# Block 2 of a two-block fp32 network: value tiles taken in pairs, and two transpositions side by side

## What is computed

```python
for i in range(DEPTH_2):
    kind, j = i % N_MIXERS, i // N_MIXERS
    h = rms_norm(x, norm_g[i]) * (1.0 + sc[:, None]) + sh[:, None]
    hc = rms_norm(xc, norm_g[i]) * (1.0 + scc) + shc
    u, z = jnp.split(h @ w_in, [n_mix_cols], axis=-1)   # u holds q, k and v
    ...
    logits = jnp.einsum("bqhgd,bkhd->bhgqk", qb, k).astype(jnp.float32) * scale
    p = jax.nn.softmax(logits, axis=-1).astype(v.dtype)
    return jnp.einsum("bhgqk,bkhd->bqhgd", p, v)
    ...
    x = x + gt[:, None] * ((o * jax.nn.silu(z)) @ w_out)
```

## Time and profile before

| | us |
|---|---|
| median of 3 runs | 2225.64 (2219.51 to 2228.34) |
| the profiled execution | 2225.83 |
| its span in the profile | 2223.7 |
| TensorE busy | 2028.1 |
| VectorE, ScalarE, GpSimd busy | 1194.2, 1089.7, 924.8 |
| block 2 within the span | from about 936 on |

### The profile page before, as it was taken

The page is one execution under the profiler, slowest core; times in us unless marked ns, Lnnn a source line. Parts: engine busy times, 40 slices in busy tenths (PEclk is TensorE's granted clock), DMA queues, the critical chain, the costliest instruction groups (busy, mean ns, idle before and its releaser), DMA issues.

```text
span 2223.7 us, 39126 instructions
## 1 busy us (share of the span) xinstructions
PE 2028.1 (91%) x14528; PEld 1707.4 (77%) x14528; DVE 1194.2 (54%) x2582; ACT 1089.7 (49%) x2089; POOL 924.8 (42%) x582
## 2 busy tenths in 40 slices
PE   6899899988998999888999999888899989979897
PEld 5798799988988899775666797566679766657776
DVE  6854556648645566346774205666430676633563
ACT  5353466453534665454554426444441656544553
POOL 1574378104744682033443123333311545532563
PEclk9899999998999999999999999999999999989998
DMA  7343556653435666542113332321232221123221
GB/s 263 106 151 105 190 171 193 188 189 115 151 109 171 186 191 191 169 143 76 48 39 105 123 97 66 107 65 48 86 114 95 76 76 48 48 93 108 88 82 57
DMA packets 72990, 262.89 MB, mean 118 GB/s; under 512 B 8048, under 2 KB 10224, under 8 KB 72560
## 3 DMA queue, kind: packets, MB, share of 16 engines
q1 hardware_dynamic: 71536, 256.31, 36.5%
q0 software_dynamic: 1280, 4.20, 0.6%
HBM read 259.43 MB, written 1.05 MB: 117 GB/s over the span
## 4 chain that ended last, share of the span: by engine, by line
PE 65%; DVE 12%; ACT 9%; issue 8%; POOL 5%; DMA 1%; DVEq 0%; ACTq 0%; SPq 0%; POOLq 0%
PE gemm L458 15%; PE gemm L459 14%; PE gemm L460 14%; PE gemm L740 7%; PE score L781 2%; PE tbank L696 2%; PE obank L839 2%; DVE small L1771 2%; POOL w_lo L298 1%; PE stat L703 1%; POOL rot L1976 1%; ACT pr L1347 1%; ACT w_hi L1020 1%; PE score L786 1%; PE gemm L666 1%
## 5 line engine op out<-in xcount | busy, mean ns | idle before, releaser
L298 POOL TENSOR_TENSOR w_lo<-ring,w_hi 128x1024 fp32r<-128x1024 f32 x262 | 628.9, 2403 | 655.9 <-ACT w_hi L1020 654.5
L458 PE MATMUL gemm<-g_hi,w_hi 128*128 128x256 f32 x1344 | 393.3, 293 | 29.0 <-DVE w_lo L298 10.5
L1020 ACT ACTIVATE w_hi<-ring 128x1024 fp32r<-128x1024 f32 x344 | 361.2, 1053 | 81.4 <-PE gemm L460 38.0
L458 PE MATMUL gemm<-h_hi,w_hi 128*128 128x512 f32 (+1 forms) x928 | 385.3, 415 | 4.7 <-POOL w_lo L298 4.7
L459 PE MATMUL gemm<-g_lo,w_hi 128*128 128x256 f32 x1344 | 382.6, 285 | 0.0
L460 PE MATMUL gemm<-g_hi,w_lo 128*128 128x256 f32 x1344 | 382.4, 284 | 0.0
L459 PE MATMUL gemm<-h_lo,w_hi 128*128 128x512 f32 (+1 forms) x928 | 348.4, 375 | 0.0
L460 PE MATMUL gemm<-h_hi,w_lo 128*128 128x512 f32 (+1 forms) x928 | 348.0, 375 | 0.0
L458 PEld LDWEIGHTS gemm<-g_hi,w_hi 128*128 128x128 f32 x1344 | 263.2, 196 | 48.1 <-issue 23.4
L459 PEld LDWEIGHTS gemm<-g_lo,w_hi 128*128 128x128 f32 x1344 | 263.3, 196 | 0.1
L460 PEld LDWEIGHTS gemm<-g_hi,w_lo 128*128 128x128 f32 x1344 | 263.0, 196 | 0.0
(11 more groups left out here) (306 smaller groups left out, 3543.7 us busy)
## 6 DMA issues: line engine op xcount, KB each, us to landing
ring<-wall SPq DMA_DIRECT2D x478, 512.0 KB, 3.7
r<-nbias POOLq DMA_DIRECT2D x16, 256.0 KB, 2.9
cst<-consts SPq DMA_DIRECT2D x1, 2037.0 KB, 13.2
r<-x_t SPq DMA_DIRECT2D x1, 1024.0 KB, 5.8
x<-ctx_t SPq DMA_DIRECT2D x1, 1024.0 KB, 15.7
y_t<-x SPq DMA_DIRECT2D x4, 256.0 KB, 2.4
cst<-consts SPq DMA_DIRECT2D x1, 303.5 KB, 3.5
x<-pos SPq DMA_DIRECT2D x1, 128.0 KB, 2.1
```

The costliest lines, as they stand in the source:

```text
L298: eng.tensor_tensor(w_lo[:, q % SPLITS, :, :], ring[:, t % RING, :, :], w_hi[:, q % SPLITS, :, :].bitcast(F), ALU.subtract)\
L458: pe.matmul(out, w[0][:, k, :], x[0], start=start, stop=False)
L1020: act.activation(w_hi[:, q % SPLITS, :, :], ring[:, t % RING, :, :], ACT.Copy).then_inc(S["hi_ready"], 1)
```

## The change

Value tiles are split like the others and taken two at a time (`value_pair`): the token block of h is the stationary operand, both tiles together are the 256 moving columns, and each product is three fp32r passes, 96 for a pair in place of 64 plain matmuls. The first pair runs with the eight feature chunks outermost and the four token blocks in two gemm and two score banks; later pairs use two gemm banks or the banks `t2` and `tb` by turns. `SPLITS` is 4, and `split_slots` puts the tiles of a pair side by side; the fourth buffer is the old `scratch`. `t2` is the third gemm bank, so from block 2 on two banks take turns. The first two value tiles come before the adaLN rows in the plan, and in layers of kind A the second row comes after the pair. High and low parts of h are made column by column as soon as a column is scaled; GpSimd scales all eight context columns, not four.

In attention of kinds A and B, `pair_to_keys` turns both units of the previous pair right behind the scores of this one, into `tb` and `t2`, then four `gemm_part`s run in one piece, then `values_both`. VectorE and ScalarE follow in that order. Kind C keeps its order, with two gemm banks.

The diff, cut to its core:

```diff
     put("ln", 2 * DEPTH, "RRRR" * FILL[2 * DEPTH])
     for L, kind in enumerate(KINDS):
         nk = n_kv_chunks(kind)
-        put("rms", L, "RRRR" * FILL_RMS[L])
-        put("v", L, "R" * nk)
+        put("v", L, "PP" + "RRRR" * FILL_RMS[L] + "PD" * (nk > 2) + "P" * (nk - 4))
         put("q0", L, "P")
         put("k", L, "P" * nk)
...
+def v_tile(L, j):
+
+    return AT["v", L] + j + (4 * FILL_RMS[L] if j >= 2 else 0)
...
+def split_slots():
+
+    fixed = {}
+    for L, kind in enumerate(KINDS):
+        nk = n_kv_chunks(kind)
+        for j in range(nk):
+            fixed[v_tile(L, j)] = (2 + j) % SPLITS
+        fixed[AT["q0", L]] = 2 if nk > 2 else 0
+    slots, last, held = [], 0, {}
+    for t, k in enumerate(PLAN):
+        if k != "R":
+            at = fixed.get(t, (last + 1) % (SPLITS - 1))
+            slots.append((at, held.get(at, -1)))
+            held[at] = len(slots) - 1
+            last = at
+    return slots
+
...
+        G2 = 2 * FILL[0] + DEPTH * (17 + NG + 2 * KC + KC + 2 * FILL[1] + 2 * FC + KC + 2 * FILL[2])
+        t2 = gb[2]
+
+        def gemm_bank(g):
+
+            return gb[g % 3 if g < G2 else g % 2]
...
-                    pe.wait_ge(S["bank_read"], g - 2)
+                    pe.wait_ge(S["bank_read"], g - 2 if g < G2 else max(g - 1, G2))
                 n["g"] += 1
-                return gb[g % 3]
+                return gemm_bank(g)
...
-                for _ in range(FILL_RMS[L]):
-                    run(ada_row())
+                n["tile"] += 2
+                run(ada_row())
...
-                for j in range(nk):
-                    w, out = tile(), bank()
-                    for t in range(4):
-                        if j == 0 and t == 2:
-                            pe.wait_ge(S["h_ctx"], (1 + L) * KC)
+                def value_pair(j):
+
+                    t = v_tile(L, j)
+                    split_tile(t), split_tile(t + 1)
+                    a, _ = SPLIT_SLOT[int(SPLIT_NO[t])]
+                    hi, lo = w_hi[:, a:a + 2, :, :], w_lo[:, a:a + 2, :, :]
+                    if j % 4 == 0:
+                        out = [bank(), bank()]
+                    else:
+                        pe.wait_ge(S["t_read"], n["t"])
+                        if j > 2:
+                            pe.wait_ge(S["v_ready"], vbase(L) + j - 2)
+                        out = [t2, tb]
+                    if j == 0:
+                        pe.wait_ge(S["ada_evac"], n["ada"])
+                        places = [(b, 0) for b in out + sbk]
+                    else:
+                        places = [(out[i // 2], i % 2 * 2 * P) for i in range(4)]
+
+                    def part(i, k, start):
+
+                        x, (b, o) = slice(i * P, (i + 1) * P), places[i]
+                        to = b[:, o:o + 2 * P].rearrange("p (a n) -> p a n", a=2)
+                        pe.matmul(to, h_hi[:, k, x], hi[:, :, k, :], start=start, stop=False)
+                        pe.matmul(to, h_hi[:, k, x], lo[:, :, k, :], start=False, stop=False)
+                        return pe.matmul(to, h_lo[:, k, x], hi[:, :, k, :], start=False, stop=(k == KC - 1))
+
+                    if j == 0:
                         for k in range(KC):
-                            if j == 0 and t == 0:
-                                pe.wait_ge(S["h_full"], (5 + L) * KC + k + 1)
-                            ins = pe.matmul(out[:, t * P:(t + 1) * P], h2[:, k, t * P:(t + 1) * P], w[:, k, :],
-                                            start=(k == 0), stop=(k == KC - 1))
-                    tile_done(ins)
+                            h_wait(k)
+                            for i in range(4):
+                                ins = part(i, k, k == 0)
+                    else:
+                        for i in range(4):
+                            for k in range(KC):
+                                ins = part(i, k, k == 0)
+                        n["tile"] += 2
+                    ins.then_inc(S["split_done"], 2)
+
+                for j in range(0, nk, 2):
+                    value_pair(j)
...
+                    pe.wait_ge(S["p_normed"], pbase(L) + U + 2)
+                    if c == 0 and u == 0:
+                        pe.wait_ge(S["ss_used"], kbase(L) + nk - 1)
+                    pe.wait_ge(S["t_read"], n["t"])
+                    for hh in range(2):
+                        for j in range(4):
+                            ins = pe.transpose((tb, t2)[hh][:, j * P:(j + 1) * P], pr[:, (U + hh) % 3, j * P:(j + 1) * P], ident)
+                        ins.then_inc(S["t_ready"], 1)
+                    n["t"] += 2
+                    turned_at[c, u + 1] = n["t"]
...
+                    for u in range(0, NU, 2) if kind != "C" else ():
+                        last = (c, u - 2) if u else (c - 1, NU - 2)
+                        scores(c, u)
+                        if last[0] >= 0:
+                            pair_to_keys(*last)
+                        for i in range(4):
+                            if i == (2 if NU == 4 else 0) and u == NU - 2 and c + 1 < KC:
+                                q_sums(c + 1)
+                            gemm_part()
+                        if last[0] >= 0:
+                            values_both(last[0], last[1] // 2)
...
+                n["tile"] += 2
+                ada_row_out(0)
+
+                def high(m):
+
+                    act.wait_ge(S["h_full"], (5 + L) * KC + m + 1)
+                    act.wait_ge(S["h_ctx"], L * KC + m + 1)
+                    act.activation(h_hi[:, m, :], h2[:, m, :], ACT.Copy).then_inc(S["h_hi_ready"], 1)
+
                 for m in range(KC):
                     act.wait_ge(S["normed"], (5 + L) * KC + m + 1)
                     act.activation(h2[:, m, 0:T], h2[:, m, 0:T], ACT.Identity, bias=ada[:, L, m, 0:1], scale=mod[:, m, 0:1])\
                         .then_inc(S["h_full"], 1)
...
+                for j in range(0, nk, 2):
+                    if j:
+                        n["tile"] += 2
+                    hi_parts(n["tile"] - 1 + AHEAD)
+                    act.wait_ge(S["split_done"], int(SPLIT_NO[v_tile(L, j + 1)]) + 1)
+                    for i in range(2):
+                        if j % 4 == 0:
+                            n["g"] += 1
+                            b = gemm_bank(n["g"] - 1)
+                        else:
+                            b = (t2, tb)[i]
+                        if j:
+                            seq(act.activation(vv[:, 2 * i:2 * i + 2, j * P:(j + 2) * P], b[:, :].rearrange("p (t n) -> p t n", t=2), ACT.Copy))
+                        else:
+                            act.activation(vv[:, i, 0:2 * P], b[:, 0:2 * P], ACT.Copy)
+                            seq(act.activation(vv[:, 2 + i, 0:2 * P], sbk[i][:, 0:2 * P], ACT.Copy))
+                        if j % 4 == 0:
+                            act.sem_inc(S["bank_read"], 1)
...
-                        act.wait_ge(S["t_ready"], tbase(L) + c * NU + u - 2)
+                        act.wait_ge(S["t_ready"], tbase(L) + (c * NU + u - 3) // 2 * 2 + 2)
...
+                    for u in range(0, NU, 2) if kind != "C" else ():
+                        last = (c, u - 1) if u else (c - 1, NU - 1)
+                        if NU == 4 and u == 2 and c + 1 < KC:
+                            query()
+                        if last[0] >= 0:
+                            second_keys(*last)
+                        exponential(c, u)
+                        exponential(c, u + 1)
+                        if NU == 6 and u == 2:
+                            if c + 1 < KC:
+                                query()
+                            elif slot:
...
+                for m in range(KC + 3):
+                    if m < KC:
+                        dve.tensor_tensor(h2[:, m, :], x2[:, m, :], st[:, :], ALU.mult).then_inc(S["normed"], 1)
+                    if m >= 3:
+                        dve.wait_ge(S["h_hi_ready"], n["h"] * KC + m - 2)
+                        dve.tensor_tensor(h_lo[:, m - 3, :], h2[:, m - 3, :], h_hi[:, m - 3, :].bitcast(F), ALU.subtract).then_inc(S["h_ready"], 1)
                 n["h"] += 1
+                split_to(AT["q0", L] - 1)
...
+                    for u in range(0, NU, 2) if kind != "C" else ():
+                        last = (c, u - 2) if u else (c - 1, NU - 2)
+                        biggest(c, u)
+                        biggest(c, u + 1)
+                        if last[0] >= 0:
+                            first_keys(*last)
+                        if u == OT and c:
+                            gate_out(c - 1)
+                        if NU == 6 and u == 4 and c + 1 < KC:
+                            q_end(c + 1)
+                        normalise(c, u)
+                        normalise(c, u + 1)
+                        if u == 2 and c + 1 < KC:
+                            q_start(c + 1)
+                            if NU == 4:
+                                q_end(c + 1)
```

(20 more changed lines are left out.)

141 lines of the change are left out of this document (64 added, 77 removed).

## The result

The changed kernel takes 2196.78 us (median of 4 runs, 2196.49 to 2203.45) against 2224.11 before (4 runs). The ratio is 0.9858, 95% interval 0.983 to 0.9886: faster by 1.4%, 32 us, and clear of noise. (The two medians alone are 27 us apart; the interval stands for 25 to 38 us.) The forecast was 81 us, and 2196.8 lies above the end of its range, 2186. The direction was right, the size wrong by more than half.

What follows compares the result with a forecast made beforehand. TensorE, busy 91% of the span, was taken to bound the kernel. Value projection -33, attention -59 and added waits +11 sum to -81: from 2225.83 us to 2144.6, given as 2144, range 2117 to 2186.

Steps and rivals of the forecast that it cites:

- Value projection: Value tiles taken in pairs of fp32r passes 0.113 us apart: -14.0 each in layers 1 and 2, together -33.
- that delays the squares by 2.1: Layer 0: two high parts of weights on ScalarE before the last adaLN row's evacuation cost 2.1; layer 0 still gains 2.
- Attention: Attention of layers 0, 1 and 3: steps -12, -23 and -5, their ends -19, sum -59, bounds 0 and -85.
- the floor: Attention step of layers 0 and 1 without the copy wait, with fewer joins and cheaper paired transpositions: 20.7 us.
- I take 0.25 for the second in place of 0.36: Attention steps: the second of two transpositions side by side costs 0.25 us, saving 0.11 three times a step.
- Of the 9.9 left I take 8: Layer 0's attention outside the six steps: 8 of 9.9 us idle TensorE time won, the same in layer 1.
- What it adds: Two gemm banks in place of three: waits at output tiles, adaLN columns and step 1, together +11 (3 to 20).
- that cover is gone only if their split is late (in the bound above): First value tiles loaded during the last output tile's passes: no cost in the sum, 3 us per layer in the bound.
- late normalisations: Rival: most attention pairs wait 1.5 us or so, about half the attention gain lost: 2174, chance 0.25.
- Slow passes: Rival: each new value pass waits for its own 188 ns load, ten pairs cost +37: 2215, chance 0.05.
- the chain as bound: Rival: the 9.1 us chain from scores to normalisation sets each attention pair's period, +32: 2258, chance 0.05.
- All at the floor: Rival: no waits at all, attention steps at the floor, -85: 2119, chance 0.07.

Runs made afterwards that it cites:

- joined: Changed kernel with four edits: slot_three, rows_first, the later high part in layer 1, and layer 3's split rotation; 2156.48 us, ratio 0.9691 to before.
- v_only: Changed kernel with the old attention order restored, paired value projection and two gemm banks kept; 2232.22 us against 2228.95 before, ratio 1.0009.
- two_banks: Kernel before the change with two gemm banks in place of three from block 2 on, nothing else; ratio 1.0063.
- slot_three: Changed kernel with the first q tile of layers 1 and 2 in split buffer 3 instead of 2; ratio 0.9797 to before.
- rows_first: Changed kernel with both adaLN rows of layer 0 ahead of the value pair, the pair in banks t2 and tb; ratio 0.9826 to before.
- the later high part: Changed kernel with ScalarE making the next tile's high part behind the q tile's copies in layer 1's steps; five steps 108.6 us, 116.0 in the change.
- the split rotation: Within joined: layer 3's q rotation started ahead of the first division, ended between the two; m1 to m7 73.5 us, 78.0 in the change.

## Why the prediction was wrong

Its mechanisms were mostly right; the sum failed in what it took to be hidden, and in the price of a transposition behind scores.

*Value projection, forecast -33, measured -22.* In layer 1 the passes of the later pairs start 0.114 apart (288 in 32.92 us from 1266.04), and the first pair took 13.1, for 10.9 and 2.0 of low clock forecast. From the adaLN row to the q run layer 1 won 13.75 (67.78 to 54.03), for 14.0 forecast. Layer 2 won 11.3; its first pair took 13.7 and its later ones 34.2. The stall at the outputs in front of it is not the reason for the 34.2. In each of the ten traces with pairs the later pairs run at one of two spacings, 0.1137 or 0.1181 us, from the first pass to the last: layer 1, with no such stall, has the longer one in six of the ten, layer 2 in nine. In the changed kernel both come at a granted clock of 1.00:

```profile
1266.04:1298.79 32.75, 32.75 (x290) 32.75 (x289) 0.00 (x0) 8.07 (x12) 11.92 (x5) 1.00 0.28 88
1640.70:1674.73 34.03, 34.03 (x290) 34.03 (x289) 0.00 (x0) 8.07 (x12) 11.93 (x5) 1.00 0.26 78
```

No run shows what sets it. Layer 3 won 2.4, for 3. Layer 0 lost 5 where 2 were forecast to be won. The step that failed is "that delays the squares by 2.1": the delay came (a wait of 2.87 at the last adaLN columns for 0.78 before; it lies ahead of the start mark, so it comes on top of the 5), but the costly one was behind the pair, the second row's copy at 5.75. I had priced the row's work and not the ring: four row tiles between a value pair and the q tile hold the q tile's load back, and ScalarE's copy of the row stands behind that tile's high part.

*Attention, forecast -59, measured -36.* Layer 0's steps won 9.8 for 12, layer 1's 15.8 for 23, layer 3's 1 for 5. In layers 0 and 1 one term failed, the same in each: the floor, 20.7. A step of layer 0 without any wait takes 21.4, one of layer 1 21.7 (`joined`). "I take 0.25 for the second in place of 0.36" was wrong, as it costs 0.35, and the first, now behind scores, costs 0.50 and not 0.36: 3 x (0.10 + 0.14) = 0.7. The allowance of 1.0 for stretched divisions in layer 1 was right, 1.10 per step. Nor is all of layer 1's 15.8 the new order's. Before, two of its six steps took 26.5 and 27.9 where the others took about 25.0, at granted clocks of 0.94 and 0.88 with no longer wait in them; the changed kernel has one such step, 24.4 for 22.9 at 0.93. That is some 2.8 of the 15.8. `v_only` and `two_banks` have the same two slow steps, so they may belong to the old order; no run shows what starts them. Layer 3's term had the right floor (12.2 in `joined`, 12.0 forecast) and no row for the wait that came, q's rotation; I had asked what is late next on the path of the probabilities only. The ends won 9.7 where I took 19: layer 0's came to 5.0 in front and lost 1.1 behind. The step that failed is "Of the 9.9 left I take 8", which takes nearly all of that idle time for a wait that the new order removes. Behind m7 TensorE waited 0.52 and 4.06 for turned probabilities and 0.19 for the row's copy; now it waits 3.27 for turned probabilities and 3.92 for the copy.

*What it adds, forecast +11 (3 to 20), measured about +26.* The 26 is what is left of the 32.2 when the other two are taken off; by runs of their own the bank is 16 and the buffer 13.6, which need not add exactly. This is the largest single miss. The bank waits were of the forecast size: 6.4 for q's bank (L1348), forecast 6, though layer 2's step grew by 4.4 with the low clock behind its wait of 3.1. The two banks alone cost 16. Not forecast at all was the split buffer: 13.6, by slot_three. The step that failed there is "that cover is gone only if their split is late (in the bound above)", which put it at nothing in the sum and at 3 us a layer in the bound. I had looked at whether the tile arrives in time; it does. What is late is the buffer, and what stands behind it is not the value tile but the copy of an output tile on the same engine.

The 49 us that are missing (81 forecast, 32.2 in the trace) are, rounded: value stages 11, attention steps 13, their ends 9, what was added 15. (The spans of the two profiled executions are only 28.8 apart: TensorE's start mark is 3.4 later in the changed one, 2.1 of it the delayed squares.) By ratio, slot_three and rows_first give back 13.6 and 7, the later high part 7.4 in layer 1's five steps and the split rotation 4.5. The rival "late normalisations" (2174, 0.25) has its wait in layer 1, but for one of 0.7 in layer 0; it does not explain 2197. Slow passes and the chain as bound are refuted, by the 0.114 and by layer 0's step with no wait.

One sum of the prediction does not come out. "All at the floor" is given as -85; its own terms make 14 + 30 + 8 = 52 for the steps (6 x 20.7 and 6 x 12.0 against the stretch sums), and 71 with the 19 of the ends. The floor case is then 2133 and not 2119, and the range's lower end of 2117 lay lower than its terms bear out; the measured time lies off the other end, so this is not what failed.

Left open: why layer 0's step 1 takes 25.0 in the old order with two banks and 21.9 in the new one, and what bounds the outputs behind layer 1 (about 3 us longer in `joined` than the shortest, 156.6), where repeated executions spread as much; and the two spacings of the value passes and the slow steps of layer 1.

## What to carry to other kernels

When tiles get a preparation they did not have ("R" became "P"), follow that preparation on its engine: what it waits for is one question (load, buffer), and what stands behind it in the same program is the other, and the costlier here. A fixed buffer among rotating ones needs its holder looked up in every layer; here one number decided 13.6 us. Price a merged run of matmuls by what comes right before the other kind of matmul, not by the number of changes alone.

## What was not expected of the hardware

A transposition of four 128 x 128 blocks costs 0.36 us between passes of 512 columns, 0.50 right behind scores. In layer 1 the pair's first passes, behind an idle time of 5.16 us, ran 0.213 us apart at a granted clock of 0.50, the lower of the two levels (1.2 GHz), and later ones 0.118 apart at 1.00 (2.4 GHz). The stretch up to the change, then the passes around it:

```profile
1251.84:1254.97 3.13, 3.13 (x15) 3.13 (x16) 3.13 (x6) 3.13 (x8) 2.32 (x4) 0.50 0.22 85
...
1254.97 0.41 PE L794 MATMUL gemm<-w_parts,h_lo 128*128 128x256 f32 x1
1255.18 0.32 PE L792 MATMUL gemm<-w_parts,h_hi 128*128 128x256 f32 x1
1255.34 0.28 PE L793 MATMUL gemm<-w_parts,h_hi 128*128 128x256 f32 x1
1255.45 0.28 PE L794 MATMUL gemm<-w_parts,h_lo 128*128 128x256 f32 x1
```

A long wait on TensorE can thus be paid a second time. Behind the 4.83 us wait above the granted clock was 0.80 and the next 24 passes took 7.15 us for 6.17; from the output tile ahead of the wait to the one behind it the changed kernel takes 19.2 us and `slot_three` 12.6. Of the 9.3 that the whole stretch fell by, 6.6 are thus the wait and what followed at once; 1.3 are the spacing of the later value passes (0.1181 in the one, 0.1137 in the other), which also changes without the edit, and 1.4 lie elsewhere.
